# Four homes for the weight tiles: the remainder is written over the raw words, and raw tiles are loaded two tiles later

## The reference

```python
def first_block(x, w_in, ...):                 # DEPTH = 2 layers
    for l in range(DEPTH):
        m = hybrid_mixer(rms_norm(x, ...), w_in[l], w_a[l], w_b[l], w_out[l], ...)
        x = x + rms_norm(m, norm_mix_post[l], NORM_EPS)
        f = swiglu(rms_norm(x, ...), w_gate_up[l], w_down[l])
        x = x + rms_norm(f, norm_ffn_post[l], NORM_EPS)
    return x
```

## Time and profile before

| | |
|---|---|
| median of 3 runs | 3234.73 us (3233.42 to 3234.97) |
| span of the profiled execution | 3232.1 us; no other time of that execution is given |
| busy share of the span | PE 98%, PEld 78%, DVE 43%, ACT 42%, POOL 42% |
| DMA | 333.28 MB, mean 103 GB/s |
| mean granted clock of PE | 0.997 of full speed |

### The profile page before, as it was taken

One profiled execution on the slowest core, in us unless ns is written; L12 is line 12 of the kernel. 1 busy time (PEld: TensorE's weight loads), 2 busy tenths in 40 slices (PEclk: granted clock), 3 DMA queues, 4 the chain that ended last, 5 costly groups with the idle time before them and its releaser, 6 DMA issues. The chain is left out here.

```text
span 3232.1 us, 45316 instructions
## 1 busy us (share of the span) xinstructions
PE 3169.8 (98%) x15912; PEld 2537.2 (78%) x15912; DVE 1388.0 (43%) x2604; ACT 1347.7 (42%) x2111; POOL 1349.9 (42%) x685
## 2 busy tenths in 40 slices
PE   9999999999999999999999999999999999999999
PEld 7778888788887778888788876777888867778887
DVE  5743335555416733335555424953112148531211
ACT  6765554322227765563322224453222245532222
POOL 3233333444443233334444443544444534444444
PEclk9999999999999999999999999999999999999999
DMA  3222222355522122222355523212323232122232
GB/s 142 65 75 89 88 88 79 118 187 196 183 95 87 60 87 79 84 88 91 121 198 183 181 87 113 73 34 80 96 96 104 96 114 66 40 78 97 97 102 87
DMA packets 93595, 333.28 MB, mean 103 GB/s; under 512 B 10864, under 2 KB 12080, under 8 KB 93232
## 3 DMA queue, kind: packets, MB, share of 16 engines
q1 hardware_dynamic: 91760, 325.52, 29.6%
q10 hardware_dynamic: 1728, 6.36, 0.5%
HBM read 329.69 MB, written 8.44 MB: 105 GB/s over the span
## 5 line engine op out<-in xcount | busy, mean ns | idle before, releaser
L440 POOL TENSOR_TENSOR wLo<-wring,wHi 128x1024 fp32r<-128x1024 f32 x482 | 1163.3, 2414 | 1703.1 <-ACT wHi L418 1702.9
L464 PE MATMUL psG<-hHi,wHi 128*128 128x512 f32 x2992 | 1183.4, 396 | 5.8 <-ACT whole L1913 2.0
L464 PE MATMUL psG<-hLo,wHi 128*128 128x512 f32 x2992 | 1169.9, 391 | 9.7 <-POOL hLo L489 8.7
L464 PE MATMUL psG<-hHi,wLo 128*128 128x512 f32 x2992 | 1165.4, 390 | 0.0
L418 ACT ACTIVATE wHi<-wring 128x1024 fp32r<-128x1024 f32 x482 | 510.1, 1058 | 959.9 <-PE psG L464 952.7
L464 PEld LDWEIGHTS psG<-hHi,wHi 128*128 128x128 f32 x2992 | 562.1, 188 | 143.4 <-issue 29.1
L464 PEld LDWEIGHTS psG<-hLo,wHi 128*128 128x128 f32 x2992 | 561.5, 188 | 141.3 <-POOL hLo L489 24.0
L464 PEld LDWEIGHTS psG<-hHi,wLo 128*128 128x128 f32 x2992 | 562.6, 188 | 113.4 <-issue 0.5
L464 PE MATMUL psG<-hidLo,wHi 128*128 128x512 f32 x704 | 273.9, 389 | 0.0
L464 PE MATMUL psG<-hidHi,wHi 128*128 128x512 f32 x704 | 273.9, 389 | 0.0
L464 PE MATMUL psG<-hidHi,wLo 128*128 128x512 f32 x704 | 273.9, 389 | 0.0
(11 more groups left out here) (332 smaller groups left out, 3265.0 us busy)
## 6 DMA issues: line engine op xcount, KB each, us to landing
wring<-in_w SPq DMA_DIRECT2D x490, 512.0 KB, 3.3
modw<-in_wmod SPq DMA_DIRECT2D x96, 512.0 KB, 5.5
e_copies<-e_rows ACTq DMA_DIRECT2D x8, 512.0 KB
T_tab<-e_copies SPq DMA_DIRECT2D x4, 1024.0 KB, 5.6
mask<-in_mask SPq DMA_DIRECT2D x2, 1536.0 KB, 6.0
xin_sb<-in_x SPq DMA_DIRECT2D x4, 512.0 KB, 5.3
e_copies<-e_rows ACTq DMA_DIRECT2D x8, 256.0 KB
out<-o_sb SPq DMA_DIRECT2D x4, 512.0 KB, 3.4
```

The costliest lines, as they stand in the source:

```text
L440: pool.tensor_tensor(wLo[:, c % CUTS, :, :], wring[:, c % RING, :, :], wHi[:, c % CUTS, :, :], ALU.subtract).then_inc(w_cut[c % CUTS], 1)
L464: mm = pe.matmul(psG[:, G.slot(u), :], w[:, c % CUTS, k, :], r(j), start=start and j == 0 and n == 0, stop=stop and j == len(kts) - 1 and ...
```

## The change

The places are laid out anew in the same memory. There are four homes for the rounded words and four for the raw words, and the remainder is written over the raw words of its own tile. So a home is free for another tile only after PE has finished with the tile in it. SP no longer waits for the remainder of tile c-4 but for the rounding of tile c-2 (`cut_behind`), which itself follows PE's end of tile c-4. The rounding is asked for as before, after PE's end of tile c-2 (`AHEAD = 2` has the place of `CUTS = 2`). At the end of a layer the next layer's four loads wait in the same way, the last one for the last product, and ACT's and POOL's work on the next layer's second tile goes ahead of the wait for the last product. The homes of the second layer of the second stack are turned by one, since 97 is no multiple of 4.

```diff
-CUTS = 2
+AHEAD = 2
-        w_cut = sems("w_cut", CUTS)
+        w_cut = sems("w_cut", RING)
-        wring = sb("wring", [P, RING, KT, P])
-        wHi, wLo = (sb(n, [P, CUTS, KT, P], dtype=F32R) for n in ("wHi", "wLo"))
+        at_w = region("w_words", 2 * RING * KT * P, ctx)
+        wring, wLo = at_w("wring", 0, RING, KT, P), at_w("wLo", 0, RING, KT, P, dtype=F32R)
+        wHi = at_w("wHi", RING * KT * P, RING, KT, P, dtype=F32R)
+        def home(c):
+            return (c + turned[0]) % RING
...
         def next_loads(sp, first, total=None, last_unit=None, slots=range(RING)):
             for j in slots:
                 if total is not None:
-                    old = max(c for c in range(total) if c % RING == j)
-                    sp.wait_ge(w_cut[old % CUTS], old // CUTS + 1)
+                    old = total - RING + j
+                    if old < total - AHEAD:
+                        cut_behind(sp, old)
+                    elif old < total - 1:
+                        sp.wait_ge(w_used, 2 * KT)
+                    else:
+                        sp.wait_ge(*G.is_full(last_unit))
+        def cut_behind(sp, c, i=None):
+            until(sp, w_high, c + AHEAD + 1 if i is None else i * RING + (c + AHEAD + 1))
...
         def next_chunks(sp, w, l, c, times, also=None):
-                    old = c + j - RING
-                    until(sp, w_cut[old % CUTS], i * (RING // CUTS) + (old // CUTS + 1))
+                    cut_behind(sp, c + j - RING, i)
...
-            act.activation(wHi[:, c % CUTS, :, :], wring[:, c % RING, :, :], ACT.Copy).then_inc(w_high, 1)
+            act.activation(wHi[:, home(c), :, :], wring[:, home(c), :, :], ACT.Copy).then_inc(w_high, 1)
-            pool.tensor_tensor(wLo[:, c % CUTS, :, :], wring[:, c % RING, :, :], wHi[:, c % CUTS, :, :], ALU.subtract).then_inc(w_cut[c % CUTS], 1)
+            pool.tensor_tensor(wLo[:, home(c), :, :], wring[:, home(c), :, :], wHi[:, home(c), :, :], ALU.subtract).then_inc(w_cut[c % RING], 1)
...
                     for n in range(2 * FT + 2, MODS):
                         for _ in range(2):
-                            sp.wait_ge(w_cut[c % CUTS], (c - RING) // CUTS + 1)
+                            cut_behind(sp, c - RING)
                             load_chunk(sp, w, l, c)
...
                     follow_down(act, CH1_DN, g_DN, CH1)
-                    act.wait_ge(w_used, 2 * KT)
-                    next_high(act, 0)
+                    next_high(act, 0, CH1)
+                    next_high(act, 1, CH1)
                     act.wait_ge(*G.is_full(g_DN + KT - 1))
-                    next_high(act, 1)
...
                     def chunk(c):
-                        sp.wait_ge(w_cut[c % CUTS], (c - RING) // CUTS + 1)
+                        cut_behind(sp, c - RING)
                         load_chunk(sp, w, l, c)
...
+                turned[0] += CH2 % RING
```

More of the change, by code:

```diff
@@ L375, in program, with next_loads @@
                                 for n, ch in ((0, CH1), (DEPTH * CH1, CH2)))
-        def next_loads(sp, first, total=None, slots=range(RING)):
+        def next_loads(sp, first, total=None, last_unit=None, slots=range(RING)):
             for j in slots:
                 if total is not None:
-                    old = max(c for c in range(total) if c % RING == j)
-                    sp.wait_ge(w_cut[old % CUTS], old // CUTS + 1)
-                sp.dma_start(wring[:, j, :, :], t["w"][first + j]).then_inc(next_in[min(j, CUTS)], 16)
+                    old = total - RING + j
[5 more added lines that the diff above has]
+                        sp.wait_ge(*G.is_full(last_unit))
+                sp.dma_start(wring[:, home(j + (total or 0)), :, :], t["w"][first + j]).then_inc(next_in[min(j, AHEAD)], 16)
@@ L386, in next_landed, with next_high @@
+        def cut_behind(sp, c, i=None):
+            until(sp, w_high, c + AHEAD + 1 if i is None else i * RING + (c + AHEAD + 1))
         def next_landed(sp):
-            for s in next_in[:CUTS]:
+            for s in next_in[:AHEAD]:
                 sp.wait_ge(s, 16)
-            sp.wait_ge(next_in[CUTS], 16 * (RING - CUTS))
-        def next_high(act, j):
+            sp.wait_ge(next_in[AHEAD], 16 * (RING - AHEAD))
+        def next_high(act, j, total=0):
             act.wait_ge(next_in[j], 16)
-            act.activation(wHi[:, j, :, :], wring[:, j, :, :], ACT.Copy).then_inc(next_cut[0], 1)
@@ L395, in next_rest @@
[L395 to L399, removed]
+            act.activation(wHi[:, home(j + total), :, :], wring[:, home(j + total), :, :], ACT.Copy).then_inc(next_cut[0], 1)
+        def next_rest(pool, total):
+            for j in range(AHEAD):
+                at = home(j + total)
+                pool.wait_ge(next_cut[0], j + 1)
+                pool.tensor_tensor(wLo[:, at, :, :], wring[:, at, :, :], wHi[:, at, :, :], ALU.subtract).then_inc(next_cut[1], 1)
+            pool.wait_ge(next_cut[1], AHEAD)
@@ L417, in cut_high @@
             until(act, w_full[c % RING], 16 * (c // RING + 1) if i is None else i * (16 * Kc // RING) + 16 * (c // RING + 1))
-            act.activation(wHi[:, c % CUTS, :, :], wring[:, c % RING, :, :], ACT.Copy).then_inc(w_high, 1)
+            act.activation(wHi[:, home(c), :, :], wring[:, home(c), :, :], ACT.Copy).then_inc(w_high, 1)
         def follow(act, c, u, i=None, Kc=0, Ku=0):
             until(act, *G.is_full(u, i, Ku))
-            cut_high(act, c + CUTS, i, Kc)
+            cut_high(act, c + AHEAD, i, Kc)
         def follow_down(act, c0, g0, total, behind=None):
-            for c in range(c0, total - CUTS):
+            for c in range(c0, total - AHEAD):
                 j, part = (c - c0) // 3, (c - c0) % 3
@@ L430, in follow_down @@
                     act.wait_ge(w_used, 2 * j + part + 1)
-                    cut_high(act, c + CUTS)
+                    cut_high(act, c + AHEAD)
                 else:
@@ L677, in _ @@
                     sp.dma_start(xin_sb[:, a, :], t["x"][a * P:(a + 1) * P, :]).then_inc(xin[a], 16)
-                next_loads(sp, 0, slots=range(CUTS))
+                next_loads(sp, 0, slots=range(AHEAD))
                 sp.dma_start(e_in[0:E_ROWS, :], t["e"]).then_inc(pick_in, 16)
@@ L683, in _ @@
                 sp.dma_start(vec2[:, :], t["v2"][0]).then_inc(rope_in, 16)
-                next_loads(sp, 0, slots=range(CUTS, RING))
+                next_loads(sp, 0, slots=range(AHEAD, RING))
                 sp.wait_ge(pro_row, 1)
@@ L785, in _ @@
                     next_chunks(sp, w, l, c, (CH1 - c) // RING)
[L786 removed]
+                    next_loads(sp, l * CH1 + CH1, CH1, g_DN + KT - 1)
                     sp.wait_ge(tmp_full, 4 * KT)
@@ L1011, in _ @@
                     credits(act, T)
-                    act.sem_inc(w_high, CUTS)
+                    act.sem_inc(w_high, AHEAD)
                     act.sem_inc(rms_full, 1)
@@ L2126, in _ @@
                         pool.memset(v, 1.0).then_inc(ones_full, 1)
-                    for s in w_cut:
+                    for s in w_cut[:AHEAD]:
                         pool.sem_inc(s, 1)
@@ L2131, in _ @@
                     pool.tensor_tensor(mw[:, m_pool:m_pool + 2 * P], mw[:, m_pool:m_pool + 2 * P], pool_scale[:, :], ALU.mult).then_inc(scale_full, 1)
-                    for c in range(CUTS, Z_FRONT + CUTS):
+                    for c in range(AHEAD, Z_FRONT + AHEAD):
                         cut_rest(pool, c)
```

42 lines of the change are left out of this document (21 added, 21 removed).

## The result

| | median, us | runs | ratio to before [95% interval] |
|---|---|---|---|
| kernel before, same chip | 3234.85 | 3233.42 to 3236.46 | |
| changed kernel | 3273.17 | 3268.97 to 3276.37 | 1.0119 [1.0106, 1.0131] |

What follows compares the result with a forecast made beforehand. PE, busy 98% of the span, was taken as the bound, so only what makes it wait costs time. 2 x (6.3 + 1.7 + 2.9) = 21.8 us on 3234.7 gave 3256.5 us; 8-in-10 range 3244 to 3263.

Steps and rivals of the forecast that it cites:

- Direction and cause: Whole kernel: slower, chance 0.93, since modw 47 and the second table stand behind loads that now wait longer in SP's queue.
- Down-projection, 6.3 + 1.7 per layer: First stack, before group 2: late modw 47 makes PE wait 6.3 us; a half-clock stretch after it adds 1.7.
- Both holds by POOL: Down-projection: POOL's remainder of chunk 130 holds DVE's `modv` to 872.5, that of chunk 131 its addition to 876.4.
- No wait for a weight tile: Kernel before: PE's listed waits hold none for a weight tile, so load, rounding and remainder are hidden.
- The wait in the mixing part, 2.9 us per layer: Second stack: the late second table delays PE's scores of step 13 by 2.9 us; bounds 2.1 and 5.8.
- the sentence that closed that part: Mixing part: ACT, DVE and PE wait for one another in turn, so the 2.9 us isn't given back.
- a clock term: Down-projection, after the 6.3 us wait: 1.7 us per layer for a 3.41 us stretch at clock 0.50; bounds 0 and 3.4.
- rival 5: More than the sum: second slow-clock stretch, or PE's mixing-part gap also lowers the clock; 3263 us and above, chance 0.07.
- rival 2: Layer ends: if barriers waited for POOL's moved work, 10.4 us come back, 3246.1 us; chance 0.04.
- rival 4: Remainder written over its input takes say 3.4 us, short tiles wait, 31 us more, 3288 us; chance 0.04.
- Homes and landings priced at nothing: All tiles: rounding and remainder keep count, size and engine; 8.4 us remain for a 3.3 us landing; price nothing.
- the prediction's own working, 1.7 us: Down-projection: modw 47 could land at most 1.7 us later, by 864.1, without making PE wait for the bank.

Runs made afterwards that it cites:

- e3: Changed kernel with the second table issued before the loads of chunks 21 and 22 and modw 46 and 47 before those of 130 and 131: 3234.17 us, 1.0003.
- e9: Kernel before, old homes, with only SP's waits ahead of raw-tile loads placed as in the changed kernel, in both stacks' loops: 3269.87 us, 1.0110.
- e7: Kernel before with modw 46 and 47 issued only after the roundings of chunks 127 and 129: 3239.70 us, 1.0018.
- e10: Changed kernel with the second table, modw 46 and 47, and DVE's two memsets all moved early: 3234.07 us, 1.0001.
- e2: Changed kernel with modw 46 and 47 issued before the loads of chunks 130 and 131: 3258.33 us, 1.0079.
- e4: Changed kernel with 16 useless products of 128 columns where PE waits in the mixing part: 3256.43 us, 1.0068.
- e5: Changed kernel with DVE's two memsets done before its last four multiplies in the down-projection: 3262.46 us, 1.0090.
- e8: Kernel before with the second table and modw 46 and 47 all issued late, after the roundings the changed kernel's loads wait for: 3260.05 us, 1.0082.
- e6: Kernel before with the second table issued only after the rounding of chunk 20: 3252.45 us, 1.0062.

## Why the prediction was wrong

- **Direction and cause: right.** The loss is the order of SP's queue and two transfers in it (e3, e9).
- **Down-projection, 6.3 + 1.7 per layer: right.** Measured 5.85 and, from chunk 129 to 132, (886.20 - 877.68) - 0.75 = 7.8 in all, of which 6.0 is PE's later start (878.80 - 872.04 - 0.75) and 1.8 the clock. Both holds by POOL came as forecast, except that the first one caught the copy of 128 x 4 ahead of `modv`, not `modv`; `modw` landed 4.1 us after its issue, not 4.6. By a rule of the Trainium skill (SBUF — State Buffer, "Who interferes with whom") plain copies and `tensor_scalar` of DVE can take the port pair that GpSimd needs, and lines with two SBUF inputs contend with GpSimd's reads. The trace agrees: the copy took 2.23 us here and 0.17 in e7.
- **The 0.75 us ahead of the wait: not forecast.** It came in one layer, from the remainder at 854.27 that DVE's multiply held. The prediction reckoned with POOL behind DVE's multiply only at chunk 130 (rightly: 870.05 + 2.65 = 872.70, and 872.5 was forecast). e3 and e10 have such a wait too, 0.42 us, and the time of before, so it counts for little; e2 and e9 don't have it.
- **"No wait for a weight tile": misread.** The full list of PE's waits in the kernel before has 1.2 us for remainders, in 2 waits. Nothing of the sum rests on it.
- **The wait in the mixing part, 2.9 us per layer: right, 3.0,** and by the steps given, with one more inside: DVE's `tensor_scalar` at 2128.76, held to 2.34 us (0.43 before) by the remainder that had moved there, so that PE waits first for `y_pool`.
- **The failed step is the sentence that closed that part:** it priced the mixing part at the wait alone, with no term and no bound for the clock. I had put a clock term behind a wait of 6.3 us in dense products and none behind one of 2.9 us in a sparse stage, and left the fall to rival 5, at 0.07. Measured in the profiled execution: 10.9 and 15.2 us, of which 7.9 and 12.0 are the clock (e4). The rows that should have warned were those of the stage itself: PE there has short products and now and then waits for DVE, its busy time in the 3.41 us ahead of the scores was only 2.91 already, and the moved work takes it to 2.07. The bound to write was a stretch at half clock for as long as the short products last. Before, that is from 2115.75 to the next product of a weight tile at 2145.40, 29.7 us with little idle time of PE, so at half speed up to some 27 us more in each layer. That bound is wide, and it would have held the time; that the stretch would last only 20 to 27 us could not be read from the kernel before.
- **"Ends give back" (rival 2): no.** The moved roundings changed nothing: PE's wait behind the barrier is 2.9 us before and after, and e3 and e10 have the time of before. **Remainder in place slower (rival 4): no,** 2.395 against 2.396 us.
- **Homes and landings priced at nothing: right** (e3, 1.0003).

The runs of the changed kernel differ by 7.4 us among themselves, those of before by 3.0. The stretches at half clock were 20.5 and 27.3 us long in its profile and 20.5 and 17.1 in e9's, so their length isn't fixed. The clearest case is e2, which has only the mixing parts' loss: its runs took 3250.1, 3254.1, 3262.5 and 3262.7 us at a mean granted clock of 0.993, 0.992, 0.990 and 0.990. A difference of 0.003 of the span is, as an estimate, some 20 us more at half clock and 10 us lost, near the 12 measured. Why a stretch lasts 27 us in one layer and 20 in the other is open.

## What to carry to other kernels

When a wait of a queue is moved, price everything that stands behind it in that queue: here the tiles had 8 us to spare, and `modw`, by the prediction's own working, 1.7 us where it was moved by 6.4. A delay on PE in a stage of short products had two prices in this kernel, the wait (3 us) and the clock after it (8 to 12 us). So write a term for the clock behind every new wait of PE, with the rest of such a stage at half clock as its bound. If the wait can't be removed, try useless products in it: here 16 of 128 columns kept the clock up, and the scores behind them came at the same time as without.

## What the runs showed of the hardware

- In the mixing part the clock fell to half after 3.41 us in which PE was busy 2.07, and then stayed at half for 17 to 27 us (10 in one case, e2) in which PE was busy 85 to 97% of the time by the trace; from the scores of step 13 on its rows show no idle time at all. The Trainium skill (TensorE: Matmul & The Clock Gate, "Part 1: The HAM clock gate") describes half rate as the resting state that activity releases. The trace agrees that the fall came with idle time of PE (1.36 us ahead of 2131.58); but here PE worked at half rate without idle time from 2135.13 to 2151.85, 16.7 us, before the full rate came back.
- In the down-projection, dense products, the clock came back 3.5 to 4.4 us after the wait's end (882.28 - 878.80 = 3.5 in the changed kernel, 879.23 - 875.31 = 3.9 in e5, 4.4 in e8). Behind a wait of 1.83 us came a stretch of 3.41 us at half (e7: 873.04 to 876.45); so it was in four of the five waits of that length in the profiles of e3, e7 and e8, and not in the fifth.
- POOL's remainder and a DVE line that meet run one after the other, whichever starts first: a DVE copy of 128 x 4 values was held to 2.23 us by POOL (0.17 free), a `tensor_scalar` of 128 x 512 took 2.34 us (0.43 free), and a remainder was held to 3.37 us by DVE's multiply (2.40 free).
- 512 KB landed 3.5 us after its issue with nothing right ahead (e7), and 4.1 to 4.2 behind another 512 KB issued 0.4 us earlier (changed kernel, e9). The table, 1 MB, took 6.1 behind a raw tile and 5.2 and 5.9 without one (e6). By the estimate that the prediction gave from the Trainium skill (SBUF — State Buffer, "The DMA setup-cost knee") the two behind another transfer would be 4.0 and 5.2: near for the first, 0.9 short for the second.
